# A streaming encoder layer: 64x64 level products, an earlier copy of the cached keys, an earlier turn of the mixed rows, and a third home for expert weights

## The reference, cut to what matters

```python
z = rmsnorm(y, norm1_w) @ w_in                       # 1024 -> 3584
qa, ka, va, qr, kr, logf, ir, gr = ...               # two groups of 4 heads
# group A, differential attention: two maps of 64 columns a head, chunk mask of 64
p = softmax(q @ k.T * 64**-0.5 + mask); oa = (p[:, :, 0] - lam * p[:, :, 1]) @ v
lam = exp(sum(lam_q1*lam_k1)) - exp(sum(lam_q2*lam_k2)) + lam_init
# group B, gated recurrence, per head and chunk
A[t, s] = sum_k q[t,k] * exp(b[t,k] - b[s,k]) * k[s,k]   for s <= t,  b = cumsum(logf)
orec = A @ ir + (q * exp(b)) @ S0;  S = exp(b_L) * S0 + (k * exp(b_L - b)).T @ ir
y = y + concat(rmsnorm(oa)*..., rmsnorm(orec)*silu(gr)) @ w_out
# experts: top-1 of 4 groups, top-2 of its 8 experts, rows sorted into blocks of 128
ys = (silu(xb @ wg[e]) * (xb @ wu[e])) @ wd[e];  y = y + sum over a row's two experts
out = rmsnorm(y, final_w)
```

## Time and profile before

| | us |
|---|---|
| median of 3 runs | 2835.92 (2834.00 to 2836.92) |
| the profiled execution's own time | 2833.84 |
| its span | 2832.1 |
| PE busy in it | 2679.2 (95%) |
| DVE busy | 1554.6 (55%) |
| ACT busy | 764.3 (27%) |
| POOL busy | 713.7 (25%) |
| mean granted clock of PE | 0.978 |

### The profile page before, as it was taken

The page is one execution under the profiler, slowest core; times in us unless marked ns, Lnnn a source line. Parts: engine busy times, 40 slices in busy tenths (PEclk is TensorE's granted clock), DMA queues, the critical chain, the costliest instruction groups (busy, mean ns, idle before and its releaser), DMA issues. The chain is left out here.

```text
span 2832.1 us, 38822 instructions
## 1 busy us (share of the span) xinstructions
PE 2679.2 (95%) x11801; PEld 1612.2 (57%) x11802; DVE 1554.6 (55%) x2860; ACT 764.3 (27%) x2102; POOL 713.7 (25%) x1001
## 2 busy tenths in 40 slices
PE   8999999999999986899999999769999999999996
PEld 6777777777777766455555555424444444444442
DVE  3565665555565564567677777624444444444442
ACT  1222222222222211555556666101111111111111
POOL 2111111111111120121222222133443433444332
PEclk9999999999999998899999999879999999999998
DMA  6000000100000028322212111389998878898785
GB/s 253 31 30 34 26 26 26 41 30 33 26 26 26 32 62 310 97 90 90 83 53 82 54 46 58 97 300 375 343 378 289 325 250 325 326 339 324 281 304 194
DMA packets 233641, 432.73 MB, mean 153 GB/s; under 512 B 31618, under 2 KB 89346, under 8 KB 233552
## 3 DMA queue, kind: packets, MB, share of 16 engines
q1 hardware_dynamic: 168080, 324.48, 32.1%
q0 software_dynamic: 30768, 94.78, 9.1%
q10 hardware_dynamic: 34704, 12.37, 1.7%
HBM read 324.77 MB, written 94.95 MB: 148 GB/s over the span
## 5 line engine op out<-in xcount | busy, mean ns | idle before, releaser
L670 PE MATMUL z_psum<-w_in_sb,hT 128*128 128x512 f32 x1088 | 480.5, 592 | 0.0
L664 PE MATMUL z_psum<-hT,w_in_sb 128*128 128x128 f32 x3264 | 374.9, 276 | 3.3 <-DMA w_in_sb<-in_w_in 3.3
L664 PEld LDWEIGHTS z_psum<-hT,w_in_sb 128*128 128x128 f32 x3264 | 370.8, 193 | 4.1 <-issue 4.1
L2072 PE MATMUL gate_psum<-w_gate_sb,block_rows_T 128*128 x720 | 320.4, 598 | 22.6 <-DMA w_gate_sb<-in_w_e_gate 22.5
L670 PEld LDWEIGHTS z_psum<-w_in_sb,hT 128*128 128x128 f32 x1088 | 200.5, 190 | 221.0 <-issue 221.0
L2086 PE MATMUL down_psum<-w_down_sb,hidden_T 128*128 x720 | 317.9, 595 | 4.7 <-DVE hidden_T L1994 4.7
L2076 PE MATMUL up_psum<-w_up_sb,block_rows_T 128*128 x720 | 316.5, 592 | 0.2
L1268 ACT ACTIVATE w_in_sb<-score_psum,neg_max 128x512 f32<-128x512 f32 (+3 forms) x320 | 197.1, 623 | 209.6 <-DVE neg_max L1355 209.5
L1939 ACT ACTIVATE square_out<-block_out 128x1024 f32<-128x1024 f32 x45 | 46.2, 1027 | 760.4 <-issue 721.8
L310 POOL TENSOR_TENSOR level_decay<-log_decay 128x256 f32<-128x256 f32 x116 | 73.5, 634 | 704.4 <-DVE level_operand L505 704.4
L2072 PEld LDWEIGHTS gate_psum<-w_gate_sb,block_rows_T 128*128 128x128 f32 x720 | 137.8, 192 | 198.0 <-issue 198.0
(11 more groups left out here) (304 smaller groups left out, 3426.2 us busy)
## 6 DMA issues: line engine op xcount, KB each, us to landing
w_gate_sb<-in_w_e_gate SPq DMA_DIRECT2D x32, 2048.0 KB, 13.2
w_up_sb<-in_w_e_up SPq DMA_DIRECT2D x32, 2048.0 KB
w_down_sb<-in_w_e_down SPq DMA_DIRECT2D x32, 2048.0 KB
w_in_sb<-in_w_in SPq DMA_DIRECT2D x7, 2048.0 KB, 18.8
hidden_by_lane<-hidden ACTq DMA_DIRECT2D x720, 16.0 KB
scratch_z<-z_ring SPq DMA_DIRECT2D x34, 256.0 KB, 2.0
scratch_y<-w_in_sb SPq DMA_DIRECT2D x17, 512.0 KB, 2.6
scratch_h<-h SPq DMA_DIRECT2D x17, 512.0 KB, 2.6
```

Source lines behind the costliest of these rows:

```text
L664: mm = pe.matmul(out[:, hd * P:(hd + 1) * P], w[:, g, c, hd * P:(hd + 1) * P], hT[:, u, c, :], start=(c == 0), stop=(c == DC - 1))
L670: mm = pe.matmul(out[:, :], hT[:, u, c, :], w[:, g, c, :], start=(c == 0), stop=(c == DC - 1))
L2072: mm = pe.matmul(gps[:, :], xT[:, u, c, :], part(wg, slot, c), start=(c == 0), stop=(c == DC - 1))
```

## The change

Four parts. In `project`, at position 1 of all tiles but the last, PE multiplies the 64 early columns of X by its 64 late ones, into the first 64 rows and the late 64 columns of the bank, and DVE copies that quarter (64x4x64) instead of the masked 128x512. In `attend_sample`, ACT copies head 0's cached keys before it waits for lambda's dot products. In `attend_mix`, `turn_m` goes into step 1's loop behind the residual, in the rounds with more than one segment (4 to 15); in the others it stays. In `experts`, each matrix has three homes, and a run's load waits for the run three before it, not two; the tables follow.

```diff
--- before.py
+++ after.py
@@ -516,6 +516,9 @@
                     chain.after(nc.vector.memset(A[:, :], 0.0))
                 if isinstance(t, int) and t == 0 and pos == 0:
                     dve.wait_ge(masks_ok, 1)
+                if pos == 1 and not is_last(t):
+                    nc.vector.tensor_copy(heads(A[:, :])[0:64, :, 64:P], heads(lps[1][:, :])[0:64, :, 64:P]).then_inc(cp_ok, 1)
+                    return
                 mk = mask[:, l:l + 1, :].to_broadcast([P, HEADS, P])
                 ins = nc.vector.copy_predicated(heads(A[:, :]), mk, heads(lps[pos % 2][:, :]))
                 ins.then_inc(cp_ok, 1)
@@ -682,7 +685,11 @@
                     left = right = X[:, (u + pos - 1) % 2, :]
                 for hd in range(HEADS):
                     c = slice(hd * P, (hd + 1) * P)
-                    mm = pe.matmul(lps[pos % 2][:, c], left[:, c], right[:, c], start=True, stop=True)
+                    if pos == 1 and not is_last(t):
+                        early, late = slice(hd * P, hd * P + 64), slice(hd * P + 64, (hd + 1) * P)
+                        mm = pe.matmul(lps[1][0:64, late], left[:, early], right[:, late], start=True, stop=True)
+                    else:
+                        mm = pe.matmul(lps[pos % 2][:, c], left[:, c], right[:, c], start=True, stop=True)
                 mm.then_inc(lv_ps, 1)
 
             def turn_kd(t):
@@ -842,15 +849,14 @@
 
         @block.scalar
         def _(act):
-            act.wait_ge(lam_e, 1)
-            nc.scalar.activation(lamd[:, 0:2], lamd[:, 2:4], ACT.Exp).then_inc(lam_e, 1)
-
             def copy_kT(h):
                 act.wait_ge(kT_ps, h + 1)
                 nc.scalar.copy(kcT[:, h % 2, :, :].rearrange("p b t -> p (b t)"),
                                kps[:, :, :].rearrange("p a n -> p (a n)")).then_inc(kT_ok, 1)
 
             copy_kT(0)
+            act.wait_ge(lam_e, 1)
+            nc.scalar.activation(lamd[:, 0:2], lamd[:, 2:4], ACT.Exp).then_inc(lam_e, 1)
             copy_kT(1)
             for h in range(HEADS):
                 u = h % 2
@@ -1203,7 +1209,7 @@
             pool.iota(q_of[:, :], [[QUEUE, N_EXP]], base=0, channel_multiplier=0, **kw)
             pool.iota(th_of[:, :], [[P, TILES]], base=0, channel_multiplier=0, **kw)
             pool.iota(me[:, :], [[0, 1]], base=1, channel_multiplier=1, **kw)
-            pool.iota(keep["run_slot"][:, :], [[0, P // 2], [-1, 2]], base=1, channel_multiplier=0)
+            pool.iota(keep["run_slot"][:, 0:P - 2], [[0, P // 3], [1, 3]], base=0, channel_multiplier=0)
             pool.memset(cnt[:, :], 0.0)
             pool.memset(glog[:, :], 4 * HIDDEN)
             pool.memset(ones[:, :], 1.0)
@@ -1476,6 +1482,8 @@
 
                 if step == 1 and there(it - 2):
                     residual(it - 2, 1)
+                if step == 1 and there(it - 1) and count(4 * it) > 1:
+                    turn_m(it - 1)
                 if step == 3 and there(it - 1) and it < LAST:
                     residual(it - 1, 0)
 
@@ -1503,7 +1511,7 @@
                     if there(it - 3):
                         norm(it - 3)
                 elif step == 1:
-                    if there(it - 1):
+                    if there(it - 1) and count(4 * it) <= 1:
                         turn_m(it - 1)
                     if there(it - 4):
                         gate(it - 4)
@@ -1569,16 +1577,17 @@
 
             chain.after(stt(out=run_row[:, :], in0=e_of[:, :], scalar=lst[:, 1:2], in1=there0, op0=ALU.is_le, op1=ALU.mult))
             chain.after(red(lists[:, 2:3], run_row[:, :], AX.X, ALU.add))
-            chain.after(ts(half[:, :], lists[:, 2:3], 0.5, -0.25, ALU.mult, ALU.add))
-            chain.after(cp(lst[:, 3:4], half[:, :]))
-            stt(out=lists[:, 3:4], in0=lst[:, 3:4], scalar=-2.0, in1=lists[:, 2:3], op0=ALU.mult, op1=ALU.add).then_inc(lst_ok, 1)
+            chain.after(ts(half[:, :], lists[:, 2:3], 1.0 / 3, -2.0 / 3, ALU.mult, ALU.add))
+            chain.after(ts(lst[:, 3:4], half[:, :], -3.0, -1.0, ALU.mult, ALU.add))
+            tt(lists[:, 3:4], lst[:, 3:4], lists[:, 2:3], ALU.add).then_inc(lst_ok, 1)
             dve.wait_ge(blk_in, 16)
             cp(blk[:, :], blk_rows[:, :])
             cp(blk4, blk_rows[:, :].rearrange("p (i r) -> p i r", r=SQ)[:, :, None, :].to_broadcast([P, LANES, LANES, SQ])).then_inc(blk_ok, 1)
             dve.wait_ge(lst_ps, 1)
             cp(keep["run_expert"][:, :], lps[0:1, 0:P])
 
-            cp(keep["run_before"][:, 1:P], lps[0:1, P:2 * P - 1])
+            nc.vector.memset(keep["run_before"][:, 0:2], 1)
+            cp(keep["run_before"][:, 2:P], lps[0:1, P:2 * P - 2])
             ts(keep["block_run"][:, :], lps[0:1, 2 * P:3 * P], 16.0, None, ALU.mult)
             cp(keep["block_slot"][:, :], lps[0:1, 3 * P:4 * P])
             dve.wait_ge(blk_ps, 1)
@@ -1734,8 +1743,8 @@
         sb = lambda n, s, d=F32: ctx.enter_context(nc.sbuf_tensor(n, s, d))
         ps = lambda n, s, d=F32: ctx.enter_context(nc.psum_tensor(n, s, d))
         sem = stage_semaphores(nc, ctx)
-        wg, wu = sb("w_gate_sb", [P, 2, DC, D_EXP]), sb("w_up_sb", [P, 2, DC, D_EXP])
-        wd = sb("w_down_sb", [P, 2, FC, D])
+        wg, wu = sb("w_gate_sb", [P, 3, DC, D_EXP]), sb("w_up_sb", [P, 3, DC, D_EXP])
+        wd = sb("w_down_sb", [P, 3, FC, D])
         slots = sb("block_slots", [P, 2], U32)
         dest = sb("block_out_rows", [P, 2], U32)
         gcol = sb("block_gates", [P, 2])
@@ -1783,8 +1792,8 @@
 
 
                 entry = lambda name, lo, hi: load(sp, keep[name][0:1, bass.ds(r, 1)], lo, hi)
-                e, slot = entry("run_expert", 0, N_EXP - 1), entry("run_slot", 0, 1)
-                if not isinstance(r, int) or r > 0:
+                e, slot = entry("run_expert", 0, N_EXP - 1), entry("run_slot", 0, 2)
+                if not isinstance(r, int) or r > 1:
                     sp.wait_ge(done, entry("run_before", 1, N_BLOCKS))
                     sp.sem_inc(sp_stand, 1)
                 wait(sp, arrived, r * 16)
@@ -2057,7 +2066,7 @@
             def run_of(b):
 
                 return (load(pe, keep["block_run"][0:1, bass.ds(b, 1)], 16, 16 * N_EXP),
-                        load(pe, keep["block_slot"][0:1, bass.ds(b, 1)], 0, 1))
+                        load(pe, keep["block_slot"][0:1, bass.ds(b, 1)], 0, 2))
 
             def part(w, slot, c, cols=slice(None)):
                 return w[:, bass.ds(slot, 1), c, cols].rearrange("p o n -> p (o n)")
```

## The result

| | before | changed |
|---|---|---|
| median of runs, us | 2835.09 (5 runs, 2834.00 to 2836.92) | 2821.58 (5 runs, 2819.19 to 2822.59) |
| ratio | | 0.9949, 95% interval 0.9937 to 0.9961 |
| the profiled execution | 2833.84 | 2819.19 |
| its span | 2832.1 | 2817.5 |

The changed kernel is 13.5 us faster, 0.5%; forecast were 17.4 (2818.5). The time lies in the range that was given.

What follows compares the result with a forecast made beforehand. PE was taken to bound the kernel nearly everywhere. The terms -3.2 - 5.0 - 4.2 - 5.0 summed to -17.4 us, from 2835.92 to 2818.5; the range ran from 2808.5 to 2830 us.

Steps and rivals of the forecast that it cites:

- What bounds it: Whole kernel: PE sets the time nearly everywhere; an edit gains from PE's own work or where PE stands still.
- The level product: `project`, position 1 of 16 tiles: PE's visit falls from 0.89 to 0.69 us, -3.2 us in all.
- The fixed price: Level product: 0.21 us added to each visit whatever its columns, taken from the scores' instruction groups.
- the first rival: Level product: stationary load doesn't shrink or changed shape costs PE twice; +3.4 instead of -3.2, 2825.1 us in all; chance 0.22.
- The merge: `project`: DVE's 0.75 us merge becomes a smaller copy; PE gains nothing, since its operand is due only next visit.
- The sample's keys: `attend_sample`: with ACT's key copy first, scores start when the query windows are there, -5.0 us.
- its cover: Stage after the sample's keys: w_out's load lands 19 us before its first use, so the 5.0 us gain is kept.
- The turn: `attend_mix`, rounds 4 to 15: an earlier turn removes PE's waits for `mix_T`; -2.0 - 4.1 + 1.9 = -4.2 us.
- the whole 4.1 goes: `attend_mix`, rounds 8 to 11: the earlier turn removes all 4.1 us of PE's wait for `mix_T`.
- The third home: `experts`: the last load is done before the tail, so its first write and read take 5.5 us less; taken as -5.0.
- The end at +3 for loads side by side: Third home, start of the experts: more early loads side by side could delay the one wanted first, bounded by +3 us.
- the slower rival: Expert stage: loads beside each block's scattered-row DMAs stretch the write-to-read loop past 20.6 us; +24, 2847.5 us; chance 0.04.

Runs made afterwards that it cites:

- the late load: The changed kernel, with the last load of down weights held until the run before the last is through, as with two homes: 2826.62 us, ratio 0.9971.
- level_twice: The kernel with only the level product changed, its four narrow products done twice in a row: 2839.97 us, ratio 1.0018.
- level_full_rows: Only the level product changed against the kernel before, with 128 stationary columns kept and 64 late ones moving: 2835.17 against 2834.69 us, ratio 1.0002.

## Why the prediction was right, point by point

- **What bounds it.** Right: PE is busy for 538.6 of 560 us of `attend_mix` and 886.6 of 887 of the expert stage in the changed kernel. Every gain was at a place where PE stood still or in PE's own work.
- **The level product, forecast -3.2, measured -1.4.** The mechanism was right and one term of its sum too small. The pace was taken as 0.060 and is 0.058. The fixed price was taken as 0.21, from the scores' groups, whose shape is another (64 rows and 128 columns of the array); for 128 rows and 64 stationary columns it is 0.34. What the first rival says, that the changed shape costs PE twice, into it and out of it, came true in kind; its size, a loss of 3.4, did not: the part is dearer than forecast and still a gain. The merge was rightly costed at nothing; the wait at position 3 is 0.29 us as before.
- **The sample's keys, forecast -5.0, measured -5.05.** Right in size and in its cover: w_out's load takes nothing back.
- **The turn, forecast -4.2, measured -2.8.** By the groups of rounds: 4 to 7 forecast -2.0, measured -1.6 (2.1 gained in step 2, 0.6 given back in step 3); 8 to 11 forecast -4.1, measured -2.0; 12 to 15 forecast +1.9, measured +0.75. The step that failed is "the whole 4.1 goes". It looked at ACT's copies in the same unit and not at what comes late next on DVE: its list up to the next unit's first maximum, unchanged in length, became the bound. For rounds 12 to 15 the new wait on the copy came where it was worked out (0.82 in round 14, with a loss of 0.25 where 0.6 was forecast).
- **The third home, forecast -5.0, measured -4.2 in the tail (-3.9 alone).** Right, and its cause is shown by the late load, but for one term: of the 5.5 us that the pair of write and read was to give, 0.8 were the read's, and the read became no shorter (5.38 after 5.11). The 0.8 to 1.3 us that the expert stage gave ahead of the tail were forecast as nothing, and whether they belong to this part is open. The end at +3 for loads side by side did not come, and neither did the slower rival: past its first runs PE waits for 0.4 us in all, on `hidden_T`.
- **The sum.** 17.4 were forecast on the profiled execution and 14.65 measured there, 14.8 by the stretches that repeat. "No part lies beside another, so they add up" was right. That the time came within 3.1 us of the forecast is in part luck: the level product and the turn together missed 3.2 us, the tail 0.8, 1.3 came unforecast in the expert stage, and the stretches that don't repeat moved by 0.7, 1.2 and -1.9 us of themselves. The range's lower end is 2808.1 by its own terms, not 2808.5, which changes nothing.

The Trainium skill, TensorE: Matmul & The Clock Gate, section "LDWEIGHTS (loading the stationary operand)", counts P/1.2 ns, by which 64 columns are 53 ns, and the pace measured with the product done twice is 58: they agree within a tenth. An estimate by it alone gave 7.4 us for the level product, five times what it gave. The Trainium skill, TensorEngine Tiling (Array Packing), section "Key Properties", says that changing the tiling mode drains TensorE; level_twice and level_full_rows agree with a cost that is paid once at a change, 0.34 us there and back, but don't show that it is a drain.

## What to carry to other kernels

A wait is worth its length only until the next engine's own list is the bound: when one is taken out, ask what that engine still has ahead of the following step, and move work that nobody waits for behind it. Here that, with the turn one segment later in the last rounds, made 2.8 us into 9.5. A smaller matmul shape among larger ones pays a fixed price at each change of shape, so narrow products pay only in longer groups. Loads that could run earlier should land before a kernel's last chain of small DMAs begins.

## What the runs showed of the hardware that was not expected

- Going from 128 to 64 stationary columns and back costs 0.34 us, and part of it shows in the timeline of the neighbours, 0.09 ahead and 0.10 behind, where no row names it.
- With 128 stationary columns, 64 moving columns cost what 128 do: 7.76 us for the visit and the group behind it, in both cases.
- An indirect write of a block took 3.4 to 3.5 us alone and 7.9 to 9.1 beside a 2 MB load; the read after it did not gain, 4.5 to 5.3 where the write had been beside the load and 5.2 to 5.4 where it had not.
- Stretches in which PE waits for loads differ by up to 4 us between executions of kernels with the same code there (38.98 to 42.90), about as much as the largest parts are worth, so a part has to be read in a stretch that repeats. Part of it is the clock: behind a wait of 3.55 us on a load the granted clock was 0.50 and 16 instructions took 3.62 us, behind one of 3.00 it was 1.00 and they took 1.95.
- At the end of `attend_mix`, behind a wait of 1.56 us that both kernels have, the clock fell in the kernel with the keys part alone (0.87 from 1755 to 1765 us) and not in before (1.00 from 1765 to 1775). Two groups of 8 instructions took 1.62 and 1.75 us instead of 1.06, and its fifth stretch is 1.4 us longer, with the same code.
